# State space rounds of a hybrid layer: a second buffer for the input maps, all output maps on GpSimd, and the low part of unit 17 behind the last modulation

## The chip, the cores and the metric

The kernel runs on one core of a Trainium2 chip. The metric is device time in microseconds (us) of one execution, as the median of several runs. The engines are TensorE (PE in the profile), VectorE (DVE), ScalarE (ACT), GpSimd (POOL) and the DMA queues that SyncE (SP) feeds. They run their own instruction streams in order and wait for each other on semaphores.

## The reference

One layer of a streaming encoder over 528 positions (16 meta tokens and 512 real ones), width 1024, everything in float32.

```python
xn = rmsnorm(h, norm1_g)
q, k, v, u, gates = split(xn @ w_in)            # 256, 256, 256, 512, 2 x 1024 columns
attn = stick_breaking_attention(rmsnorm(q), rmsnorm(k), v)      # 4 heads of 64
y = s5_ssm(u.reshape(b, l, 32, 16), ...)        # 32 groups, 64 complex states each
# x_t = abar * x_(t-1) + bbar u_t ;  y_t = Re(C x_t) + D u_t
g = gelu(y)
ssm = g * sigmoid(g @ w_glu + b_glu)
h = h + (sigmoid(gate_a) * (attn @ w_attn_proj) + sigmoid(gate_s) * (ssm @ w_ssm_proj)) @ w_o
xn = rmsnorm(h, norm2_g)
h = h + (silu(conv_g) * conv_v) @ w_down        # conv over xn @ w_up
```

## The kernel before

**The units.** The weights are worked off in 104 units of one 128-column block each. For a unit, SP loads the block, ScalarE writes its rounded high part `hi` (line 854), VectorE the remainder `lo` (line 1250, called the low part or split below), and TensorE multiplies three products (line 1737): high by high, high by low, low by high. Weights have two slots, so the low part of unit u+2 is made on VectorE in the step of unit u. Units 0 to 3 are the state space inputs, 4 and 5 the keys, 6 and 7 the queries, 8 and 9 the values, 10 to 24 and 27 the gates; unit 17 is one of the gates.

**The rounds.** The state space part is computed in chunks of 8 positions, in four rounds of 8 groups. The table `STEPS` says behind which unit each step of a round stands; every engine goes through it in the same order. For round r there are:

- the *input map* (GpSimd, `input_map`, lines 500 to 505 of the helper `cmul`): six operations over 128x512 into `g_in`, powers of abar times bbar;
- the *output map* (`map_part`, lines 474 to 476): two halves (c = 0 and 1) of three operations over 128x576 each, into one of three buffers `hout`, which lie in the tile `gates`. Rounds 0 and 1 run on GpSimd whole. In rounds 2 and 3 GpSimd makes half 1 and VectorE half 0 (`out_map`, in the steps of units 10 and 12, with `mod` as its scratch);
- `prep` r: TensorE transposes the input map (line 1835, signals `g_t`) and multiplies the output map with bpair (line 1843); ScalarE copies both out of PSUM; VectorE adds the skip term (line 1431);
- `state` r: TensorE writes the chunk inputs into PSUM (line 1857, signals `st_ps`). VectorE reads them with four products (lines 1448 to 1451, signals `st_read`, which frees the PSUM banks), and goes on with ten operations in SBUF: two sums (1453, 1454), two scans over the chunks (1456, 1457) and six that turn the states back into `xst` (1458 to 1469, signals `st_set`). These fourteen are called the modulation here;
- `readout` r: TensorE multiplies with `toep` (line 1867) and with the output map (line 1872), behind `st_set` and the DMAs that spread the taps into `toep`.

**Who waits.** TensorE's order behind unit 9 is: state 0, unit 10, prep 1, norm 3, unit 11, readout 0, state 1, unit 12, prep 2, turn of the values, unit 13, readout 1, state 2, unit 14, prep 3, turn, unit 15, readout 2, state 3, unit 16, readout 3, unit 17. The prep steps use the same PSUM banks as the state steps, so prep 2 waits for `st_read` of state 1. GpSimd's `input_map(r)` waited for `g_t` of round r-1, as there was one buffer `g_in`; its `output_map(3)` waits for `y_ps` of readout 0, which frees the buffer. Behind its maps GpSimd writes the masks of the attention (`masks_set`) and then multiplies the eight tiles of `hT` (line 821).

## Time and profile before

| | us |
|---|---|
| median of 3 runs | 730.23 |
| lowest and highest of them | 727.78, 730.58 |
| the profiled execution | 730.67 |
| its span in the trace | 729.0 |
| PE busy in it | 712.3 |

The trace is of one execution. The span runs from its first to its last instruction; the time of the execution is 1.67 us longer. Times in a timeline count from the span's start. A busy TensorE is one that has matmuls in flight, so only its idle time says where something held it up.

### The profile page before, as it was taken

The numbers are of one execution on the slowest core, as the hardware profiler recorded it, in microseconds if no ns is written. First come the engines' busy times: TensorE is split into PE (matmuls) and PEld (weight loads), VectorE is DVE, ScalarE is ACT, GpSimd is POOL, SyncE is SP. The second block draws the span as 40 slices with busy tenths as digits, with TensorE's granted clock in tenths as the row PEclk, the third lists the DMA queues.
The fourth block names the chain that finished last, engine by engine and source line by source line (L and its number), as shares of the span: only waits on it lengthen the run. The fifth ranks groups of instructions, "written<-read, shape, count | busy, mean of one in ns | idle before, by whom it ended". The sixth has DMA issues, their size and how long they took to land.

```text
span 729.0 us, 13664 instructions
## 1 busy us (share of the span) xinstructions
PE 712.3 (98%) x5384; PEld 673.2 (92%) x5384; DVE 440.6 (60%) x580; ACT 329.9 (45%) x490; POOL 177.2 (24%) x184
## 2 busy tenths in 40 slices
PE   6999999999999999999999999999999999999997
PEld 3799999999999999999999999999999998888885
DVE  4686899976779656644756666665666663232221
ACT  6646545348788655334534443343444341221120
POOL 8799975920000012233010101011010100000000
PEclk9899999999999999999999999999999999999999
DMA  8155223445311133223333222233322243333331
GB/s 226 30 161 132 68 66 71 93 97 134 98 58 59 45 87 102 87 87 88 91 106 93 86 86 86 86 93 100 95 86 86 86 120 111 96 99 94 94 94 43
DMA packets 138886, 67.86 MB, mean 93 GB/s; under 512 B 23339, under 2 KB 137231, under 8 KB 138847
## 3 DMA queue, kind: packets, MB, share of 16 engines
q1 hardware_dynamic: 138687, 67.29, 33.3%
q8 instruction: 27, 0.44, 0.3%
q14 instruction: 12, 0.10, 0.0%
q10 hardware_dynamic: 160, 0.02, 0.0%
HBM read 61.85 MB, written 4.26 MB: 91 GB/s over the span
## 4 chain that ended last, share of the span: by engine, by line
PE 82%; DVE 9%; ACT 3%; SPq 2%; DMA 2%; issue 1%; ACTq 0%; POOL 0%; DVEq 0%
PE ps L1737 74%; PE ps L2028 2%; DVE lo L1250 1%; DMA raw<-in_w_in_dram 1%; ACT hi L854 1%; PE ps L1786 1%; DVE xst L1464 1%; SPq L617 1%; DMA stack<-in_ssm_d_dram 1%; SPq L515 1%; PE ps L1907 1%; PE ps L1965 1%; SPq L608 1%; PE ps L1867 1%; PE ps L1872 1%
## 5 line engine op out<-in xcount | busy, mean ns | idle before, releaser
L1737 PE MATMUL ps<-xh,hi 128*128 128x258 f32 (+1 forms) x1088 | 222.5, 285 | 1.3 <-DVE lo L1250 0.8
L854 ACT ACTIVATE hi<-raw 128x1024 fp32r<-128x1024 f32 (+2 forms) x102 | 111.5, 1093 | 247.4 <-PE ps L1737 238.7
L1250 DVE TENSOR_TENSOR lo<-raw,hi 128x1024 fp32r<-128x1024 f32 (+2 forms) x102 | 137.6, 1349 | 138.9 <-ACT hi L854 138.3
L1737 PE MATMUL ps<-xh,lo 128*128 128x258 f32 (+1 forms) x1088 | 220.3, 284 | 0.0
L1737 PE MATMUL ps<-xl,hi 128*128 128x258 f32 (+1 forms) x1088 | 219.5, 283 | 0.0
L1737 PEld LDWEIGHTS ps<-xh,hi 128*128 128x128 f32 x1088 | 169.0, 190 | 2.7 <-DVE lo L1250 1.0
L1737 PEld LDWEIGHTS ps<-xh,lo 128*128 128x128 f32 x1088 | 169.1, 190 | 0.0
L1737 PEld LDWEIGHTS ps<-xl,hi 128*128 128x128 f32 x1088 | 169.0, 189 | 0.0
L837 POOL TENSOR_TENSOR cv<-cv 128x512 f32<-128x512 f32 x22 | 28.4, 1293 | 230.1 <-DVE cv L1695 230.1
L1684 DVE TENSOR_TENSOR ut<-ps,rb 128x516 f32<-128x516 f32 x44 | 30.6, 696 | 65.9 <-PE ps L1737 65.9
L1737 PE MATMUL ps<-ah,hi 128*128 128x512 f32 x176 | 70.4, 400 | 0.0
L1695 DVE SCALAR_TENSOR_TENSOR cv<-ut,cols,cv 128x512 f32<-128x512 f32 x88 | 65.9, 749 | 6.4 <-ACT cv L1200 0.9
L1737 PE MATMUL ps<-ah,lo 128*128 128x512 f32 x176 | 69.4, 394 | 0.0
L1737 PE MATMUL ps<-al,hi 128*128 128x512 f32 x176 | 69.4, 394 | 0.0
L824 POOL TENSOR_TENSOR ma<-ma,mb 128x516 f32<-128x516 f32 x8 | 10.8, 1353 | 140.3 <-DVE mb L1640 140.3
L1737 PEld LDWEIGHTS ps<-ah,lo 128*128 128x128 f32 x176 | 33.0, 188 | 8.2
L1737 PEld LDWEIGHTS ps<-al,hi 128*128 128x128 f32 x176 | 33.1, 188 | 7.6
L1737 PEld LDWEIGHTS ps<-ah,hi 128*128 128x128 f32 x176 | 33.1, 188 | 7.5
L1200 ACT ACTIVATE cv<-ut,cols 128x512 f32<-128x512 f32 x44 | 35.4, 804 | 2.4 <-DVE ut L1684 1.7
L1207 ACT ACTIVATE cv<-cv 128x512 f32<-128x512 f32 x22 | 14.0, 635 | 34.3 <-DVE cv L1695 34.3
L1737 PE MATMUL ps<-mh,hi 128*128 128x258 f32 x128 | 26.0, 284 | 0.3 <-DVE ml L1624 0.2
L1737 PE MATMUL ps<-mh,lo 128*128 128x258 f32 x128 | 25.8, 284 | 0.0
(293 smaller groups left out, 1001.7 us busy)
## 6 DMA issues: line engine op xcount, KB each, us to landing
raw<-in_w_up_dram SPq DMA_DIRECT2D x88, 256.0 KB, 3.1
raw<-in_w_in_dram SPq DMA_DIRECT2D x52, 256.0 KB, 3.4
raw<-in_w_down_dram SPq DMA_DIRECT2D x16, 384.0 KB, 3.4
raw<-in_w_down_dram SPq DMA_DIRECT2D x16, 320.0 KB, 3.9
raw<-in_w_o_dram SPq DMA_DIRECT2D x16, 256.0 KB, 3.0
xtok<-in_x_dram SPq DMA_DIRECT2D x4, 512.0 KB, 5.5
raw<-in_w_ssm_proj_dram SPq DMA_DIRECT2D x8, 256.0 KB, 2.8
out_dram<-yt SPq DMA_DIRECT2D x8, 256.0 KB, 2.4
```

The source lines that it names most:

```text
L515: eng.dma_start(toep[p0:p0 + GH, :, GH * j:P], kern[:, :, 0:P - GH * j]).then_inc(kern_out[r], 16)
L608: sp.dma_start(uc[p0:p0 + GH, r % 2], src[j]).then_inc(u_in[r], 16)
L824: pool.tensor_tensor(ma[m % 2][:], ma[m % 2][:], mb[m % 2][:], ALU.add)\
L837: pool.tensor_tensor(cv[s][:, 1], cv[s][:, 0], cv[s][:, 1], ALU.mult)\
L854: act.activation(hi[slot][:, 0:n * P], raw[slot][:, 0:n * P], ACT.Copy)\
L1200: act.activation(cv[s][:, part], ut[s][:, part, 2:2 + SEQ], ACT.Identity, bias=cols[:, bass.ds(m + COL_CB, 1)], scale=cols[:, bass.ds(m + ...
L1207: act.activation(cv[s][:, 0], cv[s][:, 0], ACT.Silu).then_inc(silu_a, 1)
L1250: dve.tensor_tensor(lo[slot][:, 0:n * P], raw[slot][:, 0:n * P], hi[slot][:, 0:n * P].bitcast(F32), ALU.subtract)\
L1684: dve.tensor_tensor(halves(ut[s_][:, part], HLL), psum2(4 * s_ + 2 * part, HLL), halves(rb[:, 0:LL], HLL), ALU.mult).then_inc(up_v, 1)
L1695: dve.scalar_tensor_tensor(cv[s_][:, part], ut[s_][:, part, 2 + tap:2 + tap + SEQ], w, cv[s_][:, part], ALU.mult, ALU.add)\
L1737: ins = pe.matmul(o, weights[w], acts(a, c), start=start and i == 0, stop=stop and i == 2)
L2028: ins = pe.matmul(ps[:, 2 * unit + c, 0:HL], raw[unit][:, k * P:(k + 1) * P], hT[:, k, c * HL:(c + 1) * HL], start=k == 0, stop=k == KD - 1)
```

## The change

Three things are changed. The input maps get a second buffer `g_two`, which lies where `atth` and `attl` of the attention come later, so that `input_map(r)` waits for the transposes of round r-2 only, and rounds 0 and 1 for none. The output maps of rounds 2 and 3 are made whole on GpSimd: the three operations of half 0 leave VectorE's steps of units 10 and 12, and the whole output map of round 3 stands behind the input map of round 3 and not ahead of it. And in the step of unit 15 VectorE makes the low part of unit 17 behind the modulation of state 3, not ahead of it. PE's and ACT's streams have the same instructions in the same order; PE's wait for `h_dve` in prep 2 and 3 is gone.

```diff
@@ -69,6 +69,7 @@
     0, 4, 6, 8, 10, 25, 27, 28, 36, 44, 88, 104
 U_PLAIN = 2
 U_HEADS = 17
+U_LATE_LO = 15
 GATE_ORDER = (0, 1, 2, 12, 13, 14, 15, 3, 4, 5, 6, 7, 8, 9, 10, 11)
@@ -101,8 +102,8 @@
          3: [("spread", 0), ("turns", 0)], 4: [("columns", 1), ("turns", 1)],
          5: [("norm", 0)], 6: [("norm", 1)],
          7: [("prep", 0)], 8: [("norm", 2)], 9: [("state", 0)],
-         10: [("prep", 1), ("norm", 3), ("out_map", 2)], 11: [("readout", 0), ("state", 1)],
-         12: [("prep", 2), ("turn_v", 0), ("out_map", 3)], 13: [("readout", 1), ("state", 2)],
+         10: [("prep", 1), ("norm", 3)], 11: [("readout", 0), ("state", 1)],
+         12: [("prep", 2), ("turn_v", 0)], 13: [("readout", 1), ("state", 2)],
          14: [("prep", 3), ("turn_v", 1)], 15: [("readout", 2), ("state", 3)],
          16: [("readout", 3)],
          17: [("scores", 0)], 18: [("suffix", 0)], 19: [("values", 0), ("scores", 1)],
@@ -221,6 +222,9 @@
         mb = [alloc(mix, f"mb{i}", [P, LL]) for i in range(2)]
         pad = alloc(mix, "pad", [P, 4 * (L - LL)])
         v2 = alloc(mix, "v2", [P, 5, HEADS, 2 * DH], F32R)
+        maps = ExitStack()
+        g_two = alloc(maps, "g_two", [P, 2, RP, T8, GH])
+        maps.close()
         atth = alloc(mix, "atth", [P, 2, LL], F32R)
         attl = alloc(mix, "attl", [P, 2, LL], F32R)
         blocks = alloc(mix, "blocks", [P, P])
@@ -243,7 +247,8 @@
         yg = alloc(early, "yg", [P, 2 * RP, NC])
         rot = alloc(early, "rot", [P, 2, PAIRS, NC])
         decay = alloc(early, "decay", [P, PAIRS, NC])
-        g_in = alloc(early, "g_in", [P, 2, RP, T8, GH])
+        g_own = alloc(early, "g_own", [P, 2, RP, T8, GH])
+        g_in = [g_own, g_two]
         win = alloc(early, "win", [P, 2, RP * P])
         hout = [gates[:, hout_end - (HOUTS - i) * HOUT:hout_end - (HOUTS - 1 - i) * HOUT]
@@ -354,7 +359,6 @@
         decay_set = sem("decay_set")
         g_ready = sem("g_ready")
         h_pool = sem("h_pool")
-        h_dve = sem("h_dve")
         kern_raw = sem("kern_raw")
         g_t = sem("g_t")
         k_ps = sem("k_ps")
@@ -756,11 +760,11 @@
             def input_map(r):
-                if r:
-                    pool.wait_ge(g_t, r)
+                if r >= 2:
+                    pool.wait_ge(g_t, r - 1)
                 pr = slice(r * RP, (r + 1) * RP)
                 shape = [P, RP, T8, GH]
-                cmul(pool, link, both(g_in),
+                cmul(pool, link, both(g_in[r % 2]),
                      [pw[:, c, 0:T8, pr].rearrange("p n r -> p r n").unsqueeze(3)
                       .broadcast_to(shape) for c in range(2)],
                      [bb[:, c, pr, :].unsqueeze(2).broadcast_to(shape) for c in range(2)],
@@ -789,10 +793,10 @@
             pool.tensor_copy(decay[:, :, 1:NC], sm[:, S_D2, :].unsqueeze(2)
                              .broadcast_to([P, PAIRS, NC - 1])).then_inc(decay_set, 1)
             input_map(1)
-            output_map(2, (1,))
+            output_map(2, (0, 1))
             input_map(2)
-            output_map(3, (1,))
             input_map(3)
+            output_map(3, (0, 1))
             tri = pt[:, 0:P]
             link(pool.memset(tri, -1.0))
@@ -1356,15 +1360,6 @@
                 dve.scalar_tensor_tensor(xl[:, k], hT[:, k], g1[:, k:k + 1], xh[:, k].bitcast(F32),
                                          ALU.mult, ALU.subtract).then_inc(x_ready, 1)
-            def out_map(r):
-
-                if r >= HOUTS:
-                    dve.wait_ge(y_ps, r - HOUTS + 1)
-                map_part(dve, link, r, 0, mod_flat)
-                dve.nop().then_inc(h_dve, 1)
-
-            mod_flat = mod[:].rearrange("p i r c -> p (i r c)")
-
             def rounded(o, n):
                 link(dve.tensor_scalar(n, o, 1.0 / TWO_PI, ROUND_MAGIC, ALU.mult, ALU.add))
@@ -1600,7 +1595,7 @@
                 dst, w = unit_tile(unit)
                 dve.tensor_copy(halves(dst, w), psum2(2 * (unit % 2), w)).then_inc(gate_late, 1)
-            steps = {"columns": columns, "out_map": out_map, "angle": angle, "turns": turns,
+            steps = {"columns": columns, "angle": angle, "turns": turns,
                      "norm": norm, "prep": prep, "state": state, "readout": readout,
                      "scores": scores, "suffix": suffix, "values": values, "gelu": gelu,
                      "turn_v": turn_v}
@@ -1611,10 +1606,13 @@
             for unit in range(U_PROJ):
                 if unit >= U_HEADS and is_gate(unit):
                     evacuate(unit)
-                split(unit + 2, unit % 2, tiles_of(unit + 2))
+                if unit != U_LATE_LO:
+                    split(unit + 2, unit % 2, tiles_of(unit + 2))
                 for name, i in STEPS.get(unit, []):
                     if name in steps:
                         steps[name](i)
+                if unit == U_LATE_LO:
+                    split(unit + 2, unit % 2, tiles_of(unit + 2))
                 if is_glu(unit):
                     glu(unit)
                     glu_lo(unit)
@@ -1833,11 +1831,9 @@
                 for c in range(2):
                     for i in range(RP):
                         ins = pe.transpose(ps[:, 4 + c, i * P:(i + 1) * P],
-                                           g_in[:, c, i].rearrange("p j h -> p (j h)"), ident[:])
+                                           g_in[r % 2][:, c, i].rearrange("p j h -> p (j h)"), ident[:])
                 ins.then_inc(g_t, 1)
                 pe.wait_ge(h_pool, r + 1)
-                if r >= 2:
-                    pe.wait_ge(h_dve, r - 1)
                 for i in range(RP):
                     for c in range(2):
                         ins = pe.matmul(ps[0:3 * GH, 6, i * P:(i + 1) * P],
```

GpSimd's stream, from the output map of round 2 (`gates<-pw,ct`) on. Before, its half 1 alone, then the input map of round 2 (`g_in`), then the output map of round 3:

```order
L474 TENSOR_TENSOR gates<-pw,ct 128x576 [waits pool_link]
L475 TENSOR_TENSOR pt<-pw,ct 128x576 [waits pool_link]
L476 TENSOR_TENSOR gates<-gates,pt 128x576 [waits pool_link]
L500 TENSOR_TENSOR g_in<-pw,bb 128x512 [waits pool_link,g_t]
L501 TENSOR_TENSOR pt<-pw,bb 128x512 [waits pool_link]
L502 TENSOR_TENSOR g_in<-g_in,pt 128x512 [waits pool_link]
L503 TENSOR_TENSOR g_in<-pw,bb 128x512 [waits pool_link]
L504 TENSOR_TENSOR pt<-pw,bb 128x512 [waits pool_link]
L505 TENSOR_TENSOR g_in<-g_in,pt 128x512 [waits pool_link]
L474 TENSOR_TENSOR gates<-pw,ct 128x576 [waits pool_link,y_ps]
```

In the changed kernel (lines are four further down), from the second operation of half 0 on:

```order
L479 TENSOR_TENSOR pt<-pw,ct 128x576 [waits pool_link]
L480 TENSOR_TENSOR gates<-gates,pt 128x576 [waits pool_link]
L478 TENSOR_TENSOR gates<-pw,ct 128x576 [waits pool_link]
L479 TENSOR_TENSOR pt<-pw,ct 128x576 [waits pool_link]
L480 TENSOR_TENSOR gates<-gates,pt 128x576 [waits pool_link]
L504 TENSOR_TENSOR g_own<-pw,bb 128x512 [waits pool_link,g_t]
L505 TENSOR_TENSOR pt<-pw,bb 128x512 [waits pool_link]
L506 TENSOR_TENSOR g_own<-g_own,pt 128x512 [waits pool_link]
L507 TENSOR_TENSOR g_own<-pw,bb 128x512 [waits pool_link]
L508 TENSOR_TENSOR pt<-pw,bb 128x512 [waits pool_link]
L509 TENSOR_TENSOR g_own<-g_own,pt 128x512 [waits pool_link]
L504 TENSOR_TENSOR g_two<-pw,bb 128x512 [waits pool_link,g_t]
```

Three operations were put ahead of the input map of round 2. The input map of round 3 follows it at once. Its wait for `g_t` is for round 1 in place of round 2, and that of the input map of round 2 for round 0 in place of round 1.

VectorE's stream around the output map of round 2, before: the last operations of norm 3 (`gates`, `qT`), half 0 of the map, the low part of unit 13, the first reads of state 1:

```order
L1257 TENSOR_TENSOR gates<-gates 128x516 [waits dve_link]
L1258 SCALAR_TENSOR_TENSOR gates<-gates 128x516 [waits dve_link]
L1425 SCALAR_TENSOR_TENSOR qT<-qT,cols,gates 128x516 [waits dve_link]
L474 TENSOR_TENSOR gates<-pw,ct 128x576
L475 TENSOR_TENSOR mod<-pw,ct 128x576 [waits dve_link]
L476 TENSOR_TENSOR gates<-gates,mod 128x576 [waits dve_link]
L1250 TENSOR_TENSOR lo<-raw,hi 128x1024 [waits dve_link,hi_ready]
L1448 TENSOR_TENSOR mod<-ps,rot 128x264 [waits st_ps]
L1449 TENSOR_TENSOR mod<-ps,rot 128x264
```

In the changed kernel, the same place (line 1250 is 1254 there, line 1448 is 1443):

```order
L1261 TENSOR_TENSOR gates<-gates 128x516 [waits dve_link]
L1262 SCALAR_TENSOR_TENSOR gates<-gates 128x516 [waits dve_link]
L1420 SCALAR_TENSOR_TENSOR qT<-qT,cols,gates 128x516 [waits dve_link]
L1254 TENSOR_TENSOR lo<-raw,hi 128x1024 [waits hi_ready]
L1443 TENSOR_TENSOR mod<-ps,rot 128x264 [waits st_ps]
L1444 TENSOR_TENSOR mod<-ps,rot 128x264
L1445 TENSOR_TENSOR mod<-ps,rot 128x264
L1446 TENSOR_TENSOR mod<-ps,rot 128x264
```

The three operations of the map are gone and the low part of unit 13 stands right behind the norm.

VectorE's stream around the low part of unit 17 (`lo`), before: the turned values of step 14, that low part, and the reads of state 3:

```order
L1477 TENSOR_TENSOR v<-ps,v 128x4x2x64 [waits vh_set]
L1477 TENSOR_TENSOR v<-ps,v 128x2x64
L1250 TENSOR_TENSOR lo<-raw,hi 128x1024 [waits hi_ready]
L1448 TENSOR_TENSOR mod<-ps,rot 128x264 [waits st_ps]
L1449 TENSOR_TENSOR mod<-ps,rot 128x264
L1450 TENSOR_TENSOR mod<-ps,rot 128x264
```

In the changed kernel:

```order
L1472 TENSOR_TENSOR v<-ps,v 128x4x2x64 [waits vh_set]
L1472 TENSOR_TENSOR v<-ps,v 128x2x64
L1443 TENSOR_TENSOR mod<-ps,rot 128x264 [waits st_ps]
L1444 TENSOR_TENSOR mod<-ps,rot 128x264
L1445 TENSOR_TENSOR mod<-ps,rot 128x264
L1446 TENSOR_TENSOR mod<-ps,rot 128x264
```

The reads of state 3 now stand right behind the values. The low part of unit 17 came to stand behind state 3's last operation.

## Rows read from the trace of the kernel before

**Rows 1.** The page of the profile, busy time by engine.

```profile
PE 712.3 (98%) x5384; PEld 673.2 (92%) x5384; DVE 440.6 (60%) x580; ACT 329.9 (45%) x490; POOL 177.2 (24%) x184
```

**Rows 2.** Timeline of PE: start, length, line, operation, count, idle before and releaser.

```profile
110.36 1.97 PE L1867 MATMUL ps<-uc,toep 128*128 128x66 f32 x16
...
122.26 1.10 PE L1835 MATMUL ps<-ident,g_in 128*128 128x128 f32 x8 [0.90 <-DVE mod L1451]
...
132.43 1.97 PE L1867 MATMUL ps<-uc,toep 128*128 128x66 f32 x16 [0.73 <-DVE xst L1464]
...
156.24 1.20 PE L1857 MATMUL ps<-uc,win 128*64 128x66 f32 x32
...
164.53 1.97 PE L1867 MATMUL ps<-uc,toep 128*128 128x66 f32 x16 [1.12 <-DVE xst L1464]
```

**Rows 3.** Timeline of DVE over the first round's state stage (columns as above).

```profile
98.76 0.42 DVE L1448 TENSOR_TENSOR mod<-ps,rot 128x264 f32<-128x264 f32 x1
...
100.23 0.43 DVE L1453 TENSOR_TENSOR mod<-mod 128x264 f32<-128x264 f32 x1
...
102.39 1.16 DVE L1458 TENSOR_TENSOR mod<-mod,rot 128x264 f32<-128x264 f32 x1
...
110.14 1.21 DVE L1250 TENSOR_TENSOR lo<-raw,hi 128x1024 fp32r<-128x1024 f32 x1
```

**Rows 4.** Timeline of POOL, 96 to 150 us.

```profile
96.00 1.76 POOL L476 TENSOR_TENSOR gates<-gates,pt 128x576 f32<-128x576 f32 x1
101.87 1.39 POOL L500 TENSOR_TENSOR g_in<-pw,bb 128x512 f32<-128x512 f32 x1 [4.11 <-PE ps L1835]
...
114.36 1.80 POOL L474 TENSOR_TENSOR gates<-pw,ct 128x576 f32<-128x576 f32 x1 [4.43 <-PE ps L1872]
...
123.44 1.22 POOL L500 TENSOR_TENSOR g_in<-pw,bb 128x512 f32<-128x512 f32 x1 [3.67 <-PE ps L1835]
...
136.98 12.95 POOL L821 TENSOR_TENSOR hT<-hT,rb 128x528 f32<-128x528 f32 x8
```

**Rows 5.** Timeline of DVE, query norm, output map and the next low part.

```profile
111.47 0.68 DVE L1256 SCALAR_TENSOR_TENSOR gates<-gates 128x516 f32<-128x516 f32 x1
...
114.32 0.75 DVE L474 TENSOR_TENSOR gates<-pw,ct 128x576 f32<-128x576 f32 x1
...
118.62 2.22 DVE L1250 TENSOR_TENSOR lo<-raw,hi 128x1024 fp32r<-128x1024 f32 x1 [0.15 <-DVE gates L476]
```

**Rows 6.** Timeline of DVE over the third round's state stage.

```profile
139.61 1.36 DVE L1453 TENSOR_TENSOR mod<-mod 128x264 f32<-128x264 f32 x1
...
145.91 1.35 DVE L1458 TENSOR_TENSOR mod<-mod,rot 128x264 f32<-128x264 f32 x1
...
150.25 0.43 DVE L1468 TENSOR_TENSOR mod<-mod,rot 128x264 f32<-128x264 f32 x1
```

**Rows 7.** Timeline of DVE while POOL runs maps, 75 to 88 us.

```profile
75.55 2.25 DVE L1250 TENSOR_TENSOR lo<-raw,hi 128x1024 fp32r<-128x1024 f32 x1
77.81 1.64 DVE L1256 SCALAR_TENSOR_TENSOR gates<-gates 128x528 f32<-128x528 f32 x1
...
84.22 2.13 DVE L1250 TENSOR_TENSOR lo<-raw,hi 128x1024 fp32r<-128x1024 f32 x1
86.27 1.35 DVE L1431 TENSOR_TENSOR kern<-kern,skip_i 16x128 f32<-16x128 f32 x1
```

**Rows 8.** Timeline of DVE over the last round's state stage.

```profile
158.23 0.43 DVE L1448 TENSOR_TENSOR mod<-ps,rot 128x264 f32<-128x264 f32 x1
...
163.95 0.43 DVE L1464 TENSOR_TENSOR xst<-mod 128x260 f32<-128x260 f32 x1
```

**Rows 9.** Timeline of PE in the start stage.

```profile
12.14 7.39 PE L1786 MATMUL ps<-ident,xtok 16*128 16x16 f32 x34 [1.43 <-DVE xtok L1285]
```

**Rows 10.** Windows: length, busy us (instructions) per engine, PEclk, DMA share, GB/s.

```profile
14.50:15.00 0.50, 0.50 (x3) 0.29 (x3) 0.46 (x2) 0.44 (x1) 0.50 (x2) 0.69 1.11 117
...
24.50:25.00 0.50, 0.50 (x3) 0.40 (x2) 0.00 (x0) 0.49 (x2) 0.40 (x2) 0.57 0.00 0
```

## Prediction

> **What bounds the kernel now.** I read the page first: TensorE is busy for 712.3 us of a span of 729.0 us [rows 1], so the kernel is bound by TensorE, and a change that leaves its matmuls alone can only add or remove idle time of it. Next I looked in its timeline for where it idles in the state space rounds (about 95 to 170 us). There are three places [rows 2]: 0.90 us before prep 2 at 122.26, released by VectorE's last PSUM read of state 1; 0.73 us before readout 1 at 132.43, and 1.12 us before readout 3 at 164.53, both released by VectorE's last `xst`. That is 2.75 us in all, the most that a change confined to the rounds can win. Readout 0 starts at 110.36 with no idle time before it, but it has none to spare: VectorE's state 0 ends where its next instruction starts, at 110.14 [rows 2, 3].
>
> The third view is GpSimd's timeline [rows 4]. It idles three times there: 4.11 us before 101.87, 4.43 us before 114.36 and 3.67 us before 123.44. The reader should lay this beside VectorE's operations. In state 0, VectorE's first four SBUF operations (100.23 to 102.39, 0.54 us each) fall where GpSimd idles, and the six behind them (102.39 to 110.14, 1.29 us each) where it works [rows 3]. In state 2, GpSimd multiplies `hT` from 136.98 to 149.93 [rows 4], and there the same first four operations take 6.30 us (139.61 to 145.91), where state 0 took 2.16, while the eighth, at 150.25, takes 0.43 us, GpSimd having ended [rows 6]. So while GpSimd works on two-input tiles, VectorE gets about one SBUF operation through for each of GpSimd's. GpSimd's idle time isn't waste: it is when VectorE, which feeds TensorE here, runs at its own speed.
>
> **The second buffer and the whole output map of round 2.** Up to 97.76, the end of the map's half 1 [rows 4], nothing changes: `input_map(1)` comes long after the transposes of round 0. From there GpSimd goes on without its pause with three operations, the input maps of rounds 2 and 3 (twelve) and the output map of round 3 (six), as each wait is for something past by then: 21 operations in a row, at 1.3 to 1.6 us each to about 130 us. State 0's first four SBUF operations lose their quiet time. I take 6.30 us for them [rows 6], and for the other six the 7.75 us of [rows 3], since they met a busy GpSimd already: 100.23 + 6.30 + 7.75 = 114.28 as the start of VectorE's next instruction, against 110.14. TensorE starts about 0.2 us behind that point (110.14 to 110.36, and 164.38 to 164.53 where it did wait [rows 2, 8]), so at 114.5, after **4.1 us** of idle time that wasn't there. The bounds: half of the lengthening of the four, if GpSimd is let in only now and then, gives 2.1 us; the mean of the seven operations from 139.61 to 150.25, 1.52 us, for all ten gives an end at 115.4 and 5.3 us.
>
> Half 0 of the map costs GpSimd more than it cost VectorE: the same operation took 0.75 us on VectorE at 114.32 and 1.80 us on GpSimd at 114.36 [rows 4, 5]. What is removed from VectorE is 118.62 − 114.32 = 4.30 us in step 10 [rows 5], and in step 12 the half of round 3, ahead of a low part that nobody waits for. The Trainium skill ("GPSIMD Engine Reference", 4.1 Engine selection) speaks against the move: it gives elementwise work to VectorE, with GpSimd about twice as slow for two inputs. By that figure alone six operations of 0.75 us would become some 9 us on an engine that idled 12.2 us, and the move would be free; the sum here goes by the rows, in which its price is the lost pause.
>
> **The wait for st_read of state 1.** Does removing 4.30 us from step 10 help prep 2? Behind state 0 VectorE now has the low part of unit 12, the skip term, norm 3 and the low part of unit 13, and then the four reads. Before, norm 3 fell into GpSimd's second pause and took 2.85 us (111.47 to 114.32 [rows 5]). Now GpSimd doesn't pause, so I take the durations of 75.55 to 87.62, where GpSimd ran maps [rows 7]: 2.26 + 1.35 + 6.41 + 2.05 us, and 1.47 us for the reads (98.76 to 100.23 [rows 3]), 13.5 us in all: 114.28 + 13.5 = 127.8. TensorE comes there 11.0 us after the start of readout 0 (110.36 to 122.26 less 0.90 [rows 2]), at 125.5, and waits 2.4 us: **1.5 us more** than the 0.90. The bounds: none of it, 0.9 us won, if norm 3 keeps the 2.85 us; 1.5 us on top, if the four operations of the norm are held about as long as the low parts are, 2.0 us each in place of 1.6.
>
> **Readout 1.** GpSimd's maps end near 130 us, so most of state 1 then runs free of it. Its SBUF part starts at 127.8, and TensorE needs it after prep 2, the turn and unit 13, 9.4 us later (122.26 to 132.43 less 0.73 [rows 2]). Even at 1.5 us for three operations and 0.5 for seven it takes 8 us. The wait goes: **0.7 us won**. GpSimd is later done with the maps than before by nothing that matters, as it works 12.2 us of pause away for six more operations; masks and `hT` come in time.
>
> **The low part of unit 17.** State 3's reads can start when TensorE's chunk inputs end, 156.24 + 1.20 = 157.44, instead of 158.23 [rows 2, 8]. State 3 took 6.30 us from there to readout 3 (158.23 to 164.53), so readout 3 could start at 163.8, and TensorE is ready at 164.53 − 1.12 = 163.41. The wait shrinks to 0.4: **0.7 us won**. The low part itself (1.2 us) then ends near 165, and unit 17 comes behind readout 3's 3.9 us; nobody waits. The load that is gated by it is for unit 19, two units on. Hidden, at nothing.
>
> **The sum.** 4.1 + 1.5 − 0.7 − 0.7 = +4.2 us. Behind readout 3 TensorE has work back to back, so what is lost stays lost. Against the profiled execution's 730.67 that is 734.9; as the median of the runs is 730.23, I say 734.4 us, 0.6% slower. Something under 0.5% (3.65 us) is about what a measurement of this kernel cannot tell from no change, so the sum stands just past it. The bounds above give 2.1 − 0.9 − 1.4 = −0.2 at the low end and 5.3 + 3.0 − 1.4 = +6.9 at the high one, 730.0 to 737.1; the likeliest case's own range is the upper part of it, from 732 on, below which it turns into the second rival.
>
> **The rivals.**
> - *The clock falls.* In the start stage TensorE idled 1.43 us and then did transposes [rows 9], and its granted clock went from the full 2.4 GHz to the half, 1.2 GHz, in the window at 14.50 and came back in the one at 24.50, under real matmuls [rows 10]. Four idle microseconds followed by small matmuls could do the same. The stretch at half speed was some 10 us there; if it is a third of that up to all of it, half of it is lost, 1.7 to 5 us on top: 736.1 to 739.4. Against it: the gap is the only long one. Chance 0.14. The Trainium skill ("TensorE: Matmul & The Clock Gate", Why this matters for your kernels) warns of idle gaps between bursts of matmuls of about this kind; by it the clock would fall here, and no run so far shows such a gap in this stage.
> - *Half the contention.* VectorE gets in more often than once per GpSimd operation, readout 0 waits 2 us and prep 2 no longer than before: +0.6 us or so, 731 us. For it: GpSimd's operations also lengthen beside VectorE's. Chance 0.14.
> - *The other side: the waits go and nothing comes.* State 0 still ends by 110.3 because its four quiet operations are not held up, and the 4.30 us off step 10 bring prep 2's reads forward. All three waits shrink: 0.90 + 0.73 + 0.7 = 2.3 us won, 727.9 us. It decides at state 0's end: each microsecond past 110.14 is lost one for one. Against it is [rows 6]. Chance 0.12.
> - The forecast itself has 0.60.
>
> **How the numbers follow.** Of the likeliest case about three quarters lie over 0.5% slower, and all of the clock rival: 0.58. Within 0.5%: the rest of it, half contention and most of the winning rival, 0.39. Faster by over 0.5% would need more than the three waits hold: 0.03. The range leaves out the far end of the clock rival and the best of the winning one: 730.0 to 737.5.
>
> **What would show it.** In the changed kernel's trace: GpSimd without a pause from 97.8 to about 130; the operations at 100.2 at 1.4 to 1.7 us each; readout 0 near 114.5, with about 4 us idle released by `xst`; about 2.4 us before prep 2, released by `mod`; none before readout 1; 0.4 before readout 3. A state 0 that ends before 112 makes the prediction wrong, and so does a PEclk below 1.00 behind the gap.

## The result and the profile after

| | median | lowest to highest | executions |
|---|---|---|---|
| before | 729.94 us | 727.74 to 730.70 | 6 |
| changed | 735.35 us | 734.26 to 737.86 | 6 |

The ratio is 1.008 (95% interval 1.0061 to 1.0099): the change makes the kernel 5.4 us slower. The forecast was 734.4 us, 4.2 us slower, within 730.0 to 737.5. The profiled execution took 737.86 us with a span of 735.3, the longest of the six, and the account below explains 6.3 us of span, more than the median moved.

The page of the changed kernel, its busy line and the granted clock in 40 slices (each some 18 us):

```profile
PE 716.5 (97%) x5384; PEld 677.2 (92%) x5384; DVE 435.7 (59%) x574; ACT 329.7 (45%) x490; POOL 185.2 (25%) x190
...
PEclk8899997999999999999999999999999999999999
```

TensorE has 4 us more of busy time for the same matmuls, and the clock line has a 7 in the seventh slice (110 to 129 us), where the page of before has a 9. Both say that matmuls ran slower somewhere, and that is what the timeline of PE shows (start, length, line, operation, count, idle before and releaser):

```profile
114.59 3.65 PE L1863 MATMUL ps<-uc,toep 128*128 128x66 f32 x16 [4.02 <-DVE xst L1459]
118.17 3.69 PE L1868 MATMUL ps<-xst,gates 64*128 64x66 f32 x32
```

```profile
129.70 1.04 PE L1833 MATMUL ps<-ident,g_own 128*128 128x128 f32 x8
...
138.92 1.90 PE L1863 MATMUL ps<-uc,toep 128*128 128x66 f32 x16
...
170.78 1.97 PE L1863 MATMUL ps<-uc,toep 128*128 128x66 f32 x16 [0.95 <-DMA toep<-kern]
```

Readout 0 starts at 114.59 behind 4.02 us of idle time, against 110.36 without any [rows 2]. Then its two halves take 3.65 and 3.69 us where such a step takes 2.0 (the first, at 110.36, took 1.97 in [rows 2]). Prep 2 at 129.70 and readout 1 at 138.92 have no idle time before them; readout 3 has 0.95 us, released by the toep DMA and not by VectorE. The windows of the changed kernel (length, busy us per engine, PEclk, DMA share, GB/s):

```profile
108.00:112.00 4.00, 2.57 (x22) 2.36 (x20) 3.93 (x4) 1.40 (x2) 3.66 (x4) 1.00 0.00 0
112.00:116.00 4.00, 1.41 (x7) 1.44 (x7) 3.97 (x3) 1.43 (x2) 3.77 (x4) 0.70 0.01 4
116.00:120.00 4.00, 4.00 (x29) 3.88 (x28) 3.93 (x5) 0.00 (x0) 3.84 (x3) 0.50 0.46 131
120.00:124.00 4.00, 4.00 (x51) 3.75 (x50) 3.96 (x3) 1.90 (x2) 2.97 (x3) 0.52 0.12 20
124.00:128.00 4.00, 4.00 (x34) 4.00 (x34) 3.97 (x7) 0.00 (x0) 3.84 (x3) 1.00 0.43 73
```

The clock goes from 2.4 to 1.2 GHz at about 113.6, some 3 us into the idle time and 0.9 us before readout 0 starts, stays there through readout 0 and state 1, which are small matmuls, and comes back near 124, in the dense products of unit 12. From readout 0 to prep 2 TensorE needs 129.70 − 114.59 = 15.11 us, against 11.00 before the wait [rows 2]: 4.1 us lost by the clock.

The span grew by 735.3 − 729.0 = 6.3 us. From these rows and [rows 2]:

- +4.23 at readout 0 (114.59 − 110.36);
- +4.11 from there to prep 2, and −0.90 as prep 2's wait is gone;
- −0.95 from prep 2 to readout 1 (9.22 for 10.17);
- −0.24 from readout 1 to readout 3 (31.86 for 32.10).

Together that is +6.25.

VectorE and GpSimd in the changed kernel, timelines:

```profile
99.27 0.42 DVE L1443 TENSOR_TENSOR mod<-ps,rot 128x264 f32<-128x264 f32 x1
...
100.74 1.29 DVE L1448 TENSOR_TENSOR mod<-mod 128x264 f32<-128x264 f32 x1
...
106.64 1.34 DVE L1453 TENSOR_TENSOR mod<-mod,rot 128x264 f32<-128x264 f32 x1
...
114.36 2.29 DVE L1254 TENSOR_TENSOR lo<-raw,hi 128x1024 fp32r<-128x1024 f32 x1
...
117.68 0.68 DVE L1260 SCALAR_TENSOR_TENSOR gates<-gates 128x516 f32<-128x516 f32 x1
...
121.59 0.76 DVE L1420 SCALAR_TENSOR_TENSOR qT<-qT,cols,gates 128x516 f32<-128x516 f32 x1
122.26 2.24 DVE L1254 TENSOR_TENSOR lo<-raw,hi 128x1024 fp32r<-128x1024 f32 x1
124.43 0.42 DVE L1443 TENSOR_TENSOR mod<-ps,rot 128x264 f32<-128x264 f32 x1
```

```profile
98.34 2.10 POOL L478 TENSOR_TENSOR gates<-pw,ct 128x576 f32<-128x576 f32 x1
...
121.95 1.47 POOL L478 TENSOR_TENSOR gates<-pw,ct 128x576 f32<-128x576 f32 x1 [0.95 <-PE ps L1868]
...
136.46 11.45 POOL L825 TENSOR_TENSOR hT<-hT,rb 128x528 f32<-128x528 f32 x8
```

GpSimd starts half 0 of the map at 98.34 and goes on. State 0's first four SBUF operations take 5.90 us (100.74 to 106.64, before 2.16 [rows 3]), the other six 7.72 (106.64 to 114.36). Norm 3 takes 4.58 us (117.68 to 122.26), and the reads of state 1 start at 124.43.

### The profile page after: what moved, and what is told of

The parts are those of the page before. It is cut to its first block, busy times and chain, and to the rows that moved or that the text cites. A ratio compares the mean times of both kernels' runs of the same rounds, so it can differ in the third digit from the quotient of the medians.

```text
span 735.3 us, 13660 instructions
## 1 busy us (share of the span) xinstructions
PE 716.5 (97%) x5384; PEld 677.2 (92%) x5384; DVE 435.7 (59%) x574; ACT 329.7 (45%) x490; POOL 185.2 (25%) x190
## 4 chain that ended last, share of the span: by engine, by line
PE 87%; DVE 6%; ACT 3%; DMA 2%; issue 1%; SPq 1%; ACTq 0%; POOL 0%; DVEq 0%
PE ps L1735 76%; PE ps L2024 2%; PE ps L1868 1%; PE ps L1863 1%; PE ps L1784 1%; DVE lo L1254 1%; ACT hi L858 1%; PE ps L1839 1%; DMA stack<-in_ssm_d_dram 1%; SPq L519 1%; PE ps L1903 1%; PE ps L1961 1%; DMA raw<-in_w_in_dram 1%; PE ps L2136 1%; PE ps L1928 1%
## 5 line engine op out<-in xcount | busy, mean ns | idle before, releaser
L1254 DVE TENSOR_TENSOR lo<-raw,hi 128x1024 fp32r<-128x1024 f32 (+2 forms) x102 | 139.3, 1366 | 139.4 <-ACT hi L858 139.1
```

Source lines behind the costliest of these rows:

```text
L1254: dve.tensor_tensor(lo[slot][:, 0:n * P], raw[slot][:, 0:n * P], hi[slot][:, 0:n * P].bitcast(F32), ALU.subtract)\
```

## The experiments

My theory after the result had two parts. Contention: two-input operations of GpSimd beside those of VectorE lengthen state 0 by 4 us, and readout 0 waits. Clock: idle time followed by small matmuls lets TensorE's clock fall, by chance of the execution. (In the changed kernel's profiled execution it fell before the small matmuls came, so there they are not what made it fall.) The rivals were that the second buffer carries the harm, that late signals do, or that readout 0 was slow for another reason than the clock. Each comparison has its own executions of the kernel before, on the same chip. As many executions differ in their mean clock, I also compare those with a mean clock of 0.999 or 1.00: of the kernel before, 19 of 88 are such, and took 727.06 to 729.17 us. The mean clock is TensorE's granted clock over the whole execution, as a share of 2.4 GHz. The diffs leave out parts of an edit where "..." stands.

**The wait filled, on the changed kernel** (the products' results are not used).

```diff
     pe.wait_ge(kern_out[r], 16 * T8)
+    if r == 0:
+        idle_products(4)
     pe.wait_ge(st_set, r + 1)
```

> The changed kernel, with four matmuls of 128x512 into an unused PSUM bank ahead of TensorE's wait for state 0 in readout 0 (their result is not used); they fill the 4.0 us in which it idled. Theory (the wait costs 4 us, and what comes on top in the profiled run is the clock that fell behind the idle time): VectorE's state 0 still ends near 114.3 us, readout 0 still starts near 114.6, but PEclk stays at 1.00 and readout 0 with state 1 takes 5.0 us and not 9.2. Median some 2 to 3 us under the changed kernel's 735.35, about 732.5 to 733.5, with all runs close together. Rival (the clock doesn't matter, readout 0 was slow for another cause such as the data or the memory ports): readout 0 stays at 3.6 + 3.7 us, and the time at 735 or above.

Measured: 731.02 us, ratio to before 1.0019 (1.0002 to 1.0035). Timeline of PE and windows of this kernel's profiled execution:

```profile
110.47 3.59 PE L1760 MATMUL ps<-bpair,ones 128*128 128x512 f32 x8
114.60 2.00 PE L1865 MATMUL ps<-uc,toep 128*128 128x66 f32 x16 [0.54 <-DVE xst L1459]
```

```profile
112.00:116.00 4.00, 3.46 (x18) 1.97 (x16) 3.97 (x4) 1.49 (x2) 3.77 (x4) 1.00 0.00 0
116.00:120.00 4.00, 4.00 (x49) 3.81 (x50) 3.94 (x4) 0.53 (x1) 3.84 (x3) 0.68 0.44 130
```

Readout 0 starts at 114.60 as in the changed kernel, but its first part takes 2.00 us: the contention is there, the clock isn't lost yet. In this execution, the slowest of 13 at 738.6 us, the clock fell later, at about 117.4 in the second part of readout 0, and once more behind readout 3.

Nine of the 13 had a mean clock of 0.999 or more and took 730.28 to 732.29 us, mean 730.98; the six such executions of before in the same comparison took 727.53 in the mean. So **at full clock the change costs 3.5 us**, with the filler in it. The rows of the two profiled executions give 2.4 (4.23 at readout 0, −0.6 at prep 2 by the estimate further down, −0.95 and −0.24 behind it); the 1.1 between isn't accounted for.

Of the changed kernel's 12 executions none had a mean clock above 0.993. Against its own comparison it lost 5.4 us, the filled one 0.7: 4.7 us went with the filler. Not all of that need be the filler's: more of the filled executions kept their clock in the start stage too, where the filler can do nothing. An estimate without that: the changed kernel's eight executions with a mean clock of 0.990 to 0.993 took 734.7 us in the mean, 3.8 us over the nine. (Profiled executions in which the clock fell just once, those of the late low part, the three operations and the memsets below, had 0.993 or 0.994.) The theory holds for the clock, with two corrections: the filler doesn't prevent its fall in every execution, and the median came out lower, and the executions further apart, than expected.

**The second buffer alone.** VectorE keeps its halves of the output maps.

```diff
-        g_in = alloc(early, "g_in", [P, 2, RP, T8, GH])
+        g_own = alloc(early, "g_own", [P, 2, RP, T8, GH])
+        g_in = [g_own, g_two]
...
-                if r:
-                    pool.wait_ge(g_t, r)
+                if r >= 2:
+                    pool.wait_ge(g_t, r - 1)
...
```

> The kernel before, with the second buffer of the input maps alone. Theory (VectorE is slowed only while GpSimd runs two-input operations, and what decides is which of VectorE's operations meet them): the input map of round 2 now runs from 97.9 to about 106 and meets the first five operations of state 0, but the last five run free, so state 0 ends at or before 110.2 and readout 0 doesn't wait; the wait before prep 2 goes. 0 to 2 us faster than before, 728 to 730. Rival (the missing pause alone is the harm, so the second buffer carries it): state 0 ends 3 to 4 us late, readout 0 waits as long, 733 to 735.

Measured: 730.81 us, ratio 0.9995 (0.9975 to 1.0016), unclear. The trace settles the rival, though. Timeline of VectorE, then PE's places with idle time:

```profile
98.96 1.05 DVE L1457 TENSOR_TENSOR mod<-mod 128x264 f32<-128x264 f32 x1
...
104.46 1.34 DVE L1462 TENSOR_TENSOR mod<-mod,rot 128x264 f32<-128x264 f32 x1
...
107.81 1.22 DVE L1254 TENSOR_TENSOR lo<-raw,hi 128x1024 fp32r<-128x1024 f32 x1
```

```profile
119.92 1.09 PE L1839 MATMUL ps<-ident,g_own 128*128 128x128 f32 x8 [0.37 <-DVE mod L1455]
...
160.89 1.97 PE L1871 MATMUL ps<-uc,toep 128*128 128x66 f32 x16 [0.79 <-DMA toep<-kern]
```

The first four operations take 5.5 us, but as GpSimd then waits for its next buffer, the other six take 3.35 where they took 7.75 [rows 3]; state 0 takes 8.9 us in SBUF instead of 9.9. Readout 0 doesn't wait. By the trace the second buffer delays nothing, and the interval leaves room for 1.2 us of loss at most. But five of its 12 executions had a mean clock of 0.987, and only one of the 32 of before was under 0.990. In the profiled execution the clock fell behind readout 3's 0.79 us. So the shorter waits may be paid back as clock; the runs don't separate the two.

**The output maps alone**, with one buffer. (VectorE's `out_map` steps and PE's wait for `h_dve` are gone too.)

```diff
...
             input_map(1)
-            output_map(2, (1,))
+            output_map(2, (0, 1))
             input_map(2)
-            output_map(3, (1,))
             input_map(3)
+            output_map(3, (0, 1))
```

> The kernel before, with one buffer, and the output maps of rounds 2 and 3 whole on GpSimd in the order of the changed kernel. Theory: the three extra operations fill the pause before the input map of round 2, all ten operations of state 0 meet a busy GpSimd, state 0 ends near 114.3 and readout 0 waits 4.0 us, as in the changed kernel; norm 3 falls into the second pause, so prep 2 does not wait. 733 to 736. Rival (the harm needs both parts, since only they leave GpSimd no pause at all): under 1 us of wait at readout 0, 730 to 731.

Measured: 734.31 us, ratio 1.008 (1.0051 to 1.011), the changed kernel's ratio. In the profiled execution readout 0 waited 1.90 us only, half of the expected, as GpSimd, done with its map at 111.21, had to wait for its one buffer, and state 0's last two operations ran free; but the clock fell there as well:

```profile
112.45 2.51 PE L1865 MATMUL ps<-uc,toep 128*128 128x66 f32 x16 [1.90 <-DVE xst L1464]
```

```profile
112.00:114.00 2.00, 1.55 (x13) 1.58 (x13) 2.00 (x4) 1.42 (x2) 0.00 (x0) 0.93 0.04 8
114.00:116.00 2.00, 2.00 (x15) 1.88 (x16) 1.90 (x4) 0.00 (x0) 0.00 (x0) 0.50 0.49 140
```

The output maps alone are enough for the loss: less of it is wait than in the changed kernel, and the median has moved as far. Prep 2 doesn't wait, as expected.

**The late low part alone.**

```diff
-                split(unit + 2, unit % 2, tiles_of(unit + 2))
+                if unit != 15:
+                    split(unit + 2, unit % 2, tiles_of(unit + 2))
                 for name, i in STEPS.get(unit, []):
                     if name in steps:
                         steps[name](i)
+                if unit == 15:
+                    split(unit + 2, unit % 2, tiles_of(unit + 2))
```

> The kernel before, with the low part of unit 17 behind the modulation of state 3 alone. By the prediction it wins 0.7 us (729.3). By the trace of the changed kernel, where readout 3 waited 0.95 us for the DMAs that spread the taps and not for VectorE, it wins 0.2 us or nothing, since those DMAs start behind readout 2 and land some 7.4 us after it in both kernels: 729.7 to 730.0, wait of about 1 us released by the toep DMA.

Measured: 729.47 us against 730.34, ratio 0.9993 (0.9971 to 1.0016): no difference that can be told. PE's row at readout 3:

```profile
163.87 1.97 PE L1870 MATMUL ps<-uc,toep 128*128 128x66 f32 x16 [0.61 <-DMA toep<-kern]
```

The wait is 0.61 us, released by the toep DMA. That is 0.5 us under before's 1.12, but it isn't the price of the low part. Three kernels that keep the low part ahead of state 3 also wait for the toep DMA there: 0.79 us with the second buffer, 0.67 with three more operations on GpSimd and 1.07 with the halves elsewhere (both below). How long the low part holds state 3 back hangs on when ScalarE's `hi` comes: 0.79 us in before (reads at 158.23, chunk inputs done at 157.44), nothing with the three more operations (reads at 159.38, chunk inputs done at 159.34).

**Contention without the change: three more two-input operations on GpSimd, on the kernel before** (results not used).

```diff
             output_map(2, (1,))
+            extra = pt[:, 0:RP * (T8 + 1) * GH]
+            for _ in range(3):
+                link(pool.tensor_tensor(extra, extra, extra, ALU.mult))
```

> The kernel before, with three more operations on GpSimd behind half 1 of the output map of round 2: products of 128x576 of its own scratch with itself, two inputs from SBUF, results not used. Nothing else is changed, nothing waits for them but GpSimd itself. Theory (contention for SBUF between two-input operations): state 0's first four SBUF operations take about 6 us and not 2.2, state 0 ends near 114, readout 0 waits 3.5 to 4 us; 733 to 736. Rival (it is the data flow of the change, h_pool or g_t signals late): no wait at readout 0, at most 1 us, 730 to 731.

Measured: 733.22 us, ratio 1.0053 (1.0022 to 1.0083). Timelines of GpSimd and of PE:

```profile
97.03 4.17 POOL L795 TENSOR_TENSOR pt<-pt 128x576 f32<-128x576 f32 x3 [0.18 <-POOL gates L476]
```

```profile
109.76 3.65 PE L1870 MATMUL ps<-uc,toep 128*128 128x66 f32 x16 [2.93 <-DVE xst L1467]
```

VectorE's second and third operation in SBUF, in the same execution:

```profile
97.31 1.38 DVE L1457 TENSOR_TENSOR mod<-mod 128x264 f32<-128x264 f32 x1
98.72 1.53 DVE L1459 TENSOR_TENSOR_SCAN mod<-decay,mod 128x264 f32<-128x264 f32 x1
```

The first had begun at 96.96, before GpSimd's at 97.03, and took 0.43; the others take 1.38 us and more. The kernel to lay beside it is the one with the late low part, which has before's instructions up to here and whose profiled execution also kept the full clock in the start stage. Its rows:

```profile
98.24 1.14 POOL L500 TENSOR_TENSOR g_in<-pw,bb 128x512 f32<-128x512 f32 x1 [1.38 <-PE ps L1838]
```

```profile
106.58 0.43 DVE L1464 TENSOR_TENSOR xst<-mod 128x260 f32<-128x260 f32 x1
```

```profile
107.16 1.97 PE L1870 MATMUL ps<-uc,toep 128*128 128x66 f32 x16 [0.29 <-DVE xst L1464]
```

State 0's SBUF part begins at 96.96 in both; it takes 9.97 us there and 12.58 here, and readout 0 waits 0.29 us there and 2.93 here, then runs its first part at half speed in 3.65 us. The wait is under the expected 3.5 to 4. Nothing of the data flow is touched: contention alone makes both losses, the wait and the clock. These rows also show that GpSimd's pause of 4.11 us [rows 4] belongs to an execution with a slow start stage: behind a fast one it is 1.38 us.

**The control: eight memsets in the same place** (results not used).

```diff
             output_map(2, (1,))
+            extra = pt[:, 0:RP * (T8 + 1) * GH]
+            for _ in range(8):
+                link(pool.memset(extra, 0.0))
```

> The control to the run with three extra two-input operations: eight memsets of 128x576 of the same scratch in the same place, which read nothing. If what slows VectorE is GpSimd's reading from SBUF with two inputs, state 0 ends by 110.5 as before and the time is that of before, 729.5 to 731. If any work of GpSimd slows it, state 0 ends 2 us or more late and the time is 732 or more.

Measured: 730.34 us against 730.58, ratio 1.0016 (0.999 to 1.0042). Timelines of GpSimd and VectorE:

```profile
97.06 5.03 POOL L795 MEMSET pt<- 128x576 f32 x8 [0.15 <-POOL gates L476]
```

```profile
97.01 0.43 DVE L1456 TENSOR_TENSOR mod<-mod 128x264 f32<-128x264 f32 x1
97.36 0.42 DVE L1457 TENSOR_TENSOR mod<-mod 128x264 f32<-128x264 f32 x1
...
101.59 1.22 DVE L1253 TENSOR_TENSOR lo<-raw,hi 128x1024 fp32r<-128x1024 f32 x1
```

GpSimd was busy from 97.06 to 102.09, and VectorE ran all ten operations of state 0 in 4.58 us (97.01 to 101.59), 0.46 each; the second took 0.42 us where it took 1.38 beside a product. It isn't every work of GpSimd that slows VectorE: its two-input products do, its memsets don't. Whether an operation with one input would is not tested.

**The halves placed elsewhere**, all on GpSimd, with one buffer.

```diff
             output_map(2, (1,))
             input_map(2)
+            output_map(2, (0,))
             output_map(3, (1,))
             input_map(3)
+            output_map(3, (0,))
...
                     map_part(pool, link, r, c, pt)
-                pool.nop().then_inc(h_pool, 1)
+                if 0 in parts:
+                    pool.nop().then_inc(h_pool, 1)
```

> All output maps on GpSimd with one buffer, but each half 0 behind an input map, so that GpSimd keeps its pause before the input map of round 2: half 1 of map 2, input map 2, half 0 of map 2, half 1 of map 3, input map 3, half 0 of map 3. Theory: state 0 ends at 110.2 and readout 0 doesn't wait; half 0 of map 2 runs beside norm 3 and slows it by up to 3.5 us, but VectorE is free of 4.3 us, so prep 2 waits 0.9 us or less, and readout 1 doesn't wait. 728.3 to 729.9, 0 to 1.6 us under before. Rival (work moved from VectorE to GpSimd costs wherever it is put): 732 or more.

Measured: 733.09 us, ratio 1.0045 (1.002 to 1.0069). The expectation fell. The end of state 0, GpSimd's pause and the start of half 0, and PE with its clock:

```profile
108.24 1.36 DVE L1467 TENSOR_TENSOR xst<-mod 128x260 f32<-128x260 f32 x1
109.52 2.24 DVE L1253 TENSOR_TENSOR lo<-raw,hi 128x1024 fp32r<-128x1024 f32 x1
```

```profile
99.93 1.11 POOL L500 TENSOR_TENSOR g_in<-pw,bb 128x512 f32<-128x512 f32 x1 [1.45 <-PE ps L1838]
...
108.09 1.22 POOL L474 TENSOR_TENSOR gates<-pw,ct 128x576 f32<-128x576 f32 x1 [0.18 <-POOL g_in L505]
```

```profile
109.75 1.97 PE L1868 MATMUL ps<-uc,toep 128*128 128x66 f32 x16 [1.26 <-DVE xst L1467]
```

```profile
108.00:114.00 6.00, 4.74 (x51) 4.49 (x49) 5.93 (x6) 2.83 (x3) 4.77 (x3) 0.87 0.15 43
114.00:118.00 4.00, 4.00 (x44) 3.75 (x44) 3.93 (x4) 1.90 (x2) 3.15 (x2) 0.50 0.48 113
```

In this execution TensorE kept its full clock in the start stage, so prep 1 came at 98.74 us and not at 100.75 and let GpSimd go on sooner; its pause was 1.45 us long in place of 4.11 [rows 4]. But that isn't why readout 0 waited 1.26 us. The kernel with the late low part had such a start and such a pause, 1.38 us, and waited 0.29. The rest, 0.97 us, is the place: half 0 starts at 108.09, right behind the input map, and state 0's last operation, which meets it, takes 1.36 us in place of 0.43. State 0's SBUF part takes 10.94 us in place of 9.97. The clock fell behind readout 0's wait (at about 112.5), and once more behind readout 3's of 1.07 us. So by these two executions a half placed there costs 1 us at an equal clock in the start stage, and the clock's fall on top.

**Two fillers on the kernel before**, for the clock: a third product in the start stage ahead of the first transposes, one ahead of the waits of readout 3 (results not used).

```diff
-            idle_products(2)
+            idle_products(3)
...
+                if r == ROUNDS - 1:
+                    idle_products(1)
                 pe.wait_ge(kern_out[r], 16 * T8)
```

> The kernel before with two more fillers on TensorE, whose results are not used: one matmul of 128x512 ahead of the first transposes of the start stage, where it idled 1.4 us, and one ahead of the waits of readout 3, where it idled 1.1 us. Theory (the clock falls behind idle time that is followed by small matmuls, by chance of the moment): PEclk stays at 1.00 in the start stage in more executions than before, so the median moves from 730.4 towards 727.5, the level of the executions of before whose mean clock is 0.999 or 1.00. Rival (the clock falls by the transposes and small matmuls whatever the idle time): median 730 to 731.5.

Measured: 728.79 us against 730.23, ratio 0.9989 (0.9973 to 1.0005). The median went the right way, but the interval holds 1. Executions with a mean clock of 0.995 or less are rarer, 3 of 12 against 18 of 29 of before, so the clock seems to fall less often. But the fillers cost time of their own: the four with 0.999 or more took 728.46 us in the mean, the seven such of before 727.75, and in the trace prep 1 comes at 97.92 us, where it came at 97.13 with the same clock and no filler.

**The second buffer and the late low part, VectorE keeping its halves** (the edits of two experiments above together).

> The kernel before with the second buffer and the late low part of unit 17, and VectorE keeping its halves of the output maps. Theory: no wait at readout 0, the waits before prep 2 and readout 1 mostly gone, 0.8 us left before readout 3 for the toep DMAs: 1.2 us under before at the same mean clock, 728.5 to 730.5 as a median. If the clock falls more often than before, the gain is hidden in it.

Measured: 727.92 us over all 12, ratio 0.9977 (0.9958 to 0.9996). One execution took 2599.81 us; the records don't say why, and without it the median is 727.38. The other five with a mean clock of 0.999 or more took 726.25 to 727.38, 726.61 in the mean, 1.1 us under the seven such executions of before (727.75), as expected. In the profiled execution readout 0 waited 0.20 us, prep 2 still 0.90, readout 1 not at all, and readout 3 0.70 for the toep DMA.

**The same with both fillers,** the edits of the one before and of the two fillers together.

> The second buffer, the late low part of unit 17 and both fillers: what the runs so far leave of the change, with the clock looked after. Theory: 726 to 728.5, 2 to 4 us under before and 7 or more under the changed kernel. Rival (what is won in waits comes back as clock): 729.5 or more.

Measured: 726.80 us against 730.23, ratio **0.9964** (0.995 to 0.9979): 3.4 us faster than before and 8 us faster than the changed kernel (735.35 in its own comparison, 734.80 below). PE's places with idle time between 92 and 175 us:

```profile
107.96 1.97 PE L1876 MATMUL ps<-uc,toep 128*128 128x66 f32 x16 [0.30 <-DVE xst L1468]
...
119.86 1.10 PE L1842 MATMUL ps<-ident,g_own 128*128 128x128 f32 x8 [0.90 <-DVE mod L1455]
```

Of the three waits of [rows 2] only prep 2's is left, and a new one of 0.30 us stands at readout 0. 7 of its 12 executions had a mean clock of 0.999 or more; they took 726.64 us in the mean. That is no better than without the fillers (726.61), and 1.1 us under before at an equal clock; the rest of the 3.4 us is that more executions keep the clock: 4 of 12 have 0.995 or less, of before 18 of 29. What each of the four edits gives was not told apart.

**The changed kernel once more**, beside these.

> The changed kernel once more, beside the kernel before on the same chip, for the spread of its clock. 733.5 to 736 as a median, no execution under 731, since the wait of 3 to 4 us before readout 0 is in each; the executions with the highest mean clock near 731 to 734, those with the lowest near 737.

Measured: 734.80 us (733.99 to 739.60), ratio 1.0075 (1.0047 to 1.0103). The execution with the lowest mean clock, 0.984, took 739.60 us, those with 0.992 and 0.993 took 733.99 and 734.35. In its profiled execution (738.18 us) the start stage kept the full clock, and readout 0 waited 4.18 us all the same, with the clock falling behind that wait and again behind readout 3's 0.85 us.

## Why the prediction was right, and where it was not

- **State 0 and the wait before readout 0** (4.1 us, readout 0 at 114.5): 4.02 us, at 114.59. The four operations took 5.90 us (said 6.30), the six 7.72 (said 7.75), 0.4 less together; in return state 0's SBUF part began 0.5 us later (100.74 against 100.23), which the sum did not have. That two-input operations are the cause is shown by the three extra ones and the memsets.
- **The rise of 1.5 us before prep 2** was wrong, and it is one of the two steps that failed: there was no wait at all. From the end of state 0 to the end of the four reads I said 13.5 us; it was 124.43 + 1.44 − 114.36 = 11.5. I had taken norm 3 at 6.41 us [rows 7], as beside a GpSimd that never pauses; it took 4.58. Two of its four operations ran free: the last, at 121.59, in 0.76 us, as GpSimd did pause from 121.00 to 121.95 for readout 0's signal, and the first, at 117.68, in 0.68, just ahead of a GpSimd operation at 117.69. At full clock TensorE would by these rows have come at 114.59 + 11.0 = 125.6 and waited 0.3 us; with the clock lost it came at 129.70. The term should have been −0.6, 2.1 us off.
- **Readout 1** (0.7 us won): the wait went.
- **The low part of unit 17** (0.7 us won): the wait went from 1.12 to 0.95 us, 0.2 won. I had looked at VectorE alone; the toep DMAs are a second limit just behind it. The edit alone makes no difference that can be told. (The sum itself was off by a little: 157.44 + 6.30 is 163.7, which leaves a wait of 0.3 and wins 0.8.)
- **The clock** is the other step that failed. It was a rival with a chance of 0.14 and 1.7 to 5 us on top, and by the prediction's own last sentence a PEclk below 1.00 behind the gap makes it wrong; it was 0.50, and cost 4.1 us in the profiled execution. It should have stood in the forecast: it fell behind readout 0's wait in every profiled execution in which that wait was 1.26 us or more (the changed kernel twice, the maps alone, the three operations, the halves elsewhere), also behind the 0.54 us left by the filler, and at readout 0 in none with 0.30 us or less. I had made its chance hang on the length of the gap alone.
- **The total** was partly luck. In the profiled execution the clock brought +4.1 us that the sum lacked, the wait before prep 2 was 2.4 us less than the sum had, and readout 3 won 0.5 less: +6.25 where the sum had +4.2. The medians differ by 5.4. Had the clock stayed, the change would have cost 3.5 us (the filled executions) or 2.4 (the rows). The direction and the largest term, the contention, were not luck.
- **The pages.** The Trainium skill ("TensorE: Matmul & The Clock Gate", Why this matters for your kernels) warns of idle gaps between bursts of matmuls. By that rule the trace agrees for the gap of 4.02 us, during which the clock fell. The falls behind 1.26 us and less are behind gaps shorter than it warns of; there the runs decide. The Trainium skill ("SBUF — State Buffer", SBUF: two separate sides) has an exclusive lock, for which a VectorE operation with two SBUF inputs contends only with a GpSimd operation that reads SBUF. By it the trace agrees too: 1.38 us for the operation at 97.31 beside a product, 0.42 us for the same one, at 97.36, beside memsets.

## What to carry to other kernels

Before filling an engine's pause, look at what runs fastest during it: here GpSimd's pause, 4.1 us or 1.4 us as the start stage went, was VectorE's quiet time, and VectorE fed TensorE with nothing to spare. Read each wait with its second limit, or the edit that removes the first wins less than its row shows. And count a new wait in front of small matmuls for more than its length: the clock can fall behind it and cost as much again.

## What the runs showed that I had not expected

The start stage has two outcomes. In the profiled execution of before, the clock was at half from about 14.7 to 24.9 us [rows 10]. Eleven profiled executions have that stage as it was: the clock fell there in four (before, the changed kernel's first, the filled one, the maps alone), for a part of it in one (the second buffer), and not at all in six, among them the changed kernel's second. Of the 88 executions of before, those with a mean clock of 0.999 or more are some 3 us under the others.

The clock also fell behind shorter waits, now and then. At readout 3 it fell behind 0.79 us (the second buffer), 0.80 (the filled kernel), 0.85 (the changed kernel's second), 1.07 (the halves elsewhere) and 1.21 (the memsets), and at about 132 us behind readout 1's 0.73 with the late low part. But it stayed full behind readout 3's 0.67 (the three operations), 0.95 (the changed kernel's first), 1.12 (before [rows 2]) and 1.35 us (the maps alone), and behind readout 1's 0.73 in before. So the length of the wait doesn't decide it. The stretch with the memsets:

```profile
160.28 1.97 PE L1870 MATMUL ps<-uc,toep 128*128 128x66 f32 x16 [1.21 <-DVE xst L1467]
```

```profile
162.00:164.00 2.00, 2.00 (x23) 1.93 (x21) 0.00 (x0) 0.00 (x0) 0.00 (x0) 0.61 0.46 102
...
168.00:170.00 2.00, 2.00 (x14) 2.00 (x14) 1.38 (x3) 1.97 (x4) 0.00 (x0) 0.69 0.35 70
```

What decides in which execution it falls behind so short a wait stays open, and so does why 9 of 13 executions of the filled kernel had a mean clock of 0.999 or more, which hardly leaves room for a slow start stage, and 6 of 32 of before beside it: the filler comes some 85 us after the end of that stretch.
